# Down steps of a Strassen-Winograd pair: two PSUM banks in a fixed order, or five banks in a rotated order

## The reference

```
def swiglu(x, w_gate, w_up, w_down):
    return (jax.nn.silu(x @ w_gate) * (x @ w_up)) @ w_down
...
    h = x + 0.5 * swiglu(rmsnorm(x, ffn1_norm), ffn1_w_gate, ffn1_w_up, ffn1_w_down)
    p = rmsnorm(h, mix_norm) @ w_in
...
    h = h + jnp.concatenate([s_out, c_out.astype(s_out.dtype)], axis=-1) @ w_out
    h = h + 0.5 * swiglu(rmsnorm(h, ffn2_norm), ffn2_w_gate, ffn2_w_up, ffn2_w_down)
```

## Time and profile before

| | us |
|---|---|
| median of 3 runs | 1847.4 (1846.5 to 1847.51) |
| the profiled execution, whole | 1847.25 |
| its span, first to last instruction | 1845.4 |
| PE busy in it | 1792.8 (97%) |
| DVE busy | 1274.1 (69%) |
| ACT, POOL busy | 655.0, 624.0 |
| mean granted PE clock | 0.994 of full |

### The profile page before, as it was taken

One profiled execution on the slowest core, in us unless ns is written; L12 is line 12 of the kernel. 1 busy time (PEld: TensorE's weight loads), 2 busy tenths in 40 slices (PEclk: granted clock), 3 DMA queues, 4 the chain that ended last, 5 costly groups with the idle time before them and its releaser, 6 DMA issues.

```text
span 1845.4 us, 31589 instructions
## 1 busy us (share of the span) xinstructions
PE 1792.8 (97%) x11953; PEld 1751.7 (95%) x11953; DVE 1274.1 (69%) x2428; ACT 655.0 (35%) x1281; POOL 624.0 (34%) x669
## 2 busy tenths in 40 slices
PE   8999999999999999999999999899999999999998
PEld 7999999999999999999999999899999999999998
DVE  6658868677766865823774869767776686777766
ACT  7411333333333332533112455233233333333324
POOL 2787222322232222203994221233223223222321
PEclk9999999999999999999999999999999999999999
DMA  6133111111111110455114401111211111111112
GB/s 168 44 117 109 29 46 46 53 46 52 47 52 52 41 58 25 154 125 121 46 41 132 141 25 40 48 56 41 58 41 52 52 46 52 47 52 46 52 47 93
DMA packets 162502, 119.75 MB, mean 65 GB/s; under 512 B 10242, under 2 KB 156226, under 8 KB 161844
## 3 DMA queue, kind: packets, MB, share of 16 engines
q1 hardware_dynamic: 157012, 110.36, 20.3%
q0 software_dynamic: 864, 5.28, 0.9%
q10 hardware_dynamic: 4480, 2.10, 0.5%
HBM read 102.01 MB, written 15.72 MB: 64 GB/s over the span
## 4 chain that ended last, share of the span: by engine, by line
PE 92%; DVE 5%; issue 2%; ACT 1%; DMA 0%; DVEq 0%
PE bank_pair L1110 20%; PE bank_pair L1111 19%; PE bank_pair L1112 19%; PE bank_down L1110 11%; PE bank_down L1112 9%; PE bank_down L1111 9%; DVE HT L2262 1%; DVE XL L2285 1%; DVE XLX L2586 0%; PE bank_pair L1513 0%; PE bank_pair L1486 0%; PE bank_pair L1606 0%; PE bank_pair L1505 0%; DVE XTL L2574 0%; PE bank_pair L1218 0%
## 5 line engine op out<-in xcount | busy, mean ns | idle before, releaser
L2512 DVE SCALAR_TENSOR_TENSOR HT<-bank_down,HT 128x344 f32<-128x344 f32 x648 | 325.1, 513 | 166.1 <-PE bank_down L1112 163.1
L1110 PE MATMUL bank_pair<-XHM,U_hi 128*128 128x344 f32 x720 | 231.9, 322 | 1.9 <-issue 1.7
L1112 PE MATMUL bank_pair<-XHM,U_lo 128*128 128x344 f32 x720 | 230.0, 319 | 0.0
L1111 PE MATMUL bank_pair<-XLM,U_hi 128*128 128x344 f32 x720 | 229.9, 319 | 0.0
L3163 POOL TENSOR_TENSOR U_lo<-AST,U_hi 128x512 fp32r<-128x512 f32 x74 | 110.1, 1490 | 280.7 <-ACT U_hi L1670 280.7
L1110 PE MATMUL bank_pair<-XH,U_hi 128*128 128x344 f32 x608 | 195.4, 321 | 0.0
L1111 PE MATMUL bank_pair<-XL,U_hi 128*128 128x344 f32 x608 | 194.7, 320 | 0.0
L1112 PE MATMUL bank_pair<-XH,U_lo 128*128 128x344 f32 x608 | 194.5, 320 | 0.0
L1110 PE MATMUL bank_pair<-XH,WH 128*128 128x344 f32 x576 | 186.9, 325 | 4.4 <-DVE XL L2285 4.3
L1111 PE MATMUL bank_pair<-XL,WH 128*128 128x344 f32 x576 | 184.4, 320 | 0.0
L1112 PE MATMUL bank_pair<-XH,WL 128*128 128x344 f32 x576 | 184.3, 320 | 0.0
(11 more groups left out here) (375 smaller groups left out, 4583.2 us busy)
## 6 DMA issues: line engine op xcount, KB each, us to landing
DQ_raw<-in_ffn_w_down SPq DMA_DIRECT2D x52, 256.0 KB, 2.9
U_raw<-in_ffn_w_gate SPq DMA_DIRECT2D x40, 256.0 KB, 2.9
AST<-in_ffn_w_gate SPq DMA_DIRECT2D x40, 256.0 KB, 2.9
U_raw<-in_ffn_w_up SPq DMA_DIRECT2D x40, 256.0 KB, 3.3
AST<-in_ffn_w_up SPq DMA_DIRECT2D x40, 256.0 KB, 2.9
RAW<-in_w_in SPq DMA_DIRECT2D x16, 512.0 KB, 3.9
DQR<-in_ffn_w_down SPq DMA_DIRECT2D x25, 256.0 KB, 2.9
X<-in_x_prompt SPq DMA_DIRECT2D x8, 512.0 KB, 8.4
```

Source lines behind the costliest of these rows:

```text
L1110: pe.matmul(out, wh, xh, start=first, stop=False, skip_group_check=onto)
L1111: pe.matmul(out, wh, xl, start=False, stop=False, skip_group_check=onto)
L1112: return pe.matmul(out, wl, xh, start=False, stop=last, skip_group_check=onto)
L2512: dve.scalar_tensor_tensor(ht, DB[at % 2][:, 0:TW], 0.5, ht, ALU.mult, ALU.add).then_inc(pair_free, 1)
```

## The change

The steps of a quarter get a new order, M1, M5, M2, M6, M3, P1, M7, P2, and M4 goes behind M5 of the next quarter (the last M4 stands alone at the end, two steps behind the last M7). The steps use five banks in roles that change with the quarter: bank_down0 and 1, and the three banks of the up pass (bank_pair2's second half, bank_pair1's two halves), which no product uses in a gate pass. Each step waits for the add of the last step in its own bank. The up products V1a, M1 and M2 wait for the last adds on their banks. The first step goes behind product 7, and every product from there to 42 has exactly one. On DVE, an add stands two products later than its step (`ADD_LAG`); the last one falls into the up pass. The order of the hidden forms changes (`FORMS`, and `PLAIN_FORMS` for the first pair of an FFN), and on ACT three `sums_hi` move some places later.

```
-DOWN_STEPS = [((("W", A11, B11),), False, (0, 1)), ((("S", S1, T1),), False, (1, 2)),
...
-STEP_AFTER = [9 + 34 * n // STEPS for n in range(STEPS)]
-MIX_BEHIND = [len(DOWN_STEPS) * (q + 1) - 1 for q in range(3)]
+DOWN_STEPS = {"M1": ((("W", A11, B11),), False, (0, 1), 0), "M5": ((("S", S1, T1),), False, (1, 2), 1),
...
+DOWN_ORDER = []
+for _q in range(5):
+    for _name in ("M1", "M5", "M4", "M2", "M6", "M3", "P1", "M7", "P2"):
+        _at = _q - (_name == "M4")
+        if 0 <= _at < 4:
+            DOWN_ORDER.append((_at, _name))
+STEPS = len(DOWN_ORDER)
+BANK_ROLES = [(0, 1, 2, 3, 4), (2, 1, 3, 4, 0), (3, 1, 4, 0, 2), (4, 1, 0, 2, 3)]
+STEP_BANK = [BANK_ROLES[q][DOWN_STEPS[name][3]] for q, name in DOWN_ORDER]
+STEP_AFTER = [7 + n for n in range(STEPS)]
+ADD_LAG = 2
+QUARTER_LAST = [DOWN_ORDER.index((q, "M4")) for q in range(4)]
+MIX_BEHIND = QUARTER_LAST[:3]
 LOWS_BEHIND = [n + 4 for n in MIX_BEHIND]
-FORMS = [B13, B11, T1, T3, B22, B21, T4, T2, B23]
-PLAIN_FORMS = [B13, B11, T1, T3, B22, B23, B21, T4, T2]
+FORMS = [B13, B11, T1, B22, T2, B21, B23, T3, T4]
+PLAIN_FORMS = [B13, B11, T1, B22, B23, T3, B21, T2, T4]
...
+        STEP_BANKS = DB + [BANK[1][x] for x in ("v", "x", "y")]
...
-                out = bank_of(at)[:, 0:TW]
+                before = [i for i in range(n) if STEP_BANK[i] == STEP_BANK[n]]
+                if before:
+                    pe.wait_ge(pair_free, step_base(p) + before[-1] + 1)
+                elif STEP_BANK[n] >= 2:
+                    pe.wait_ge(h_raw, 6 * (p + 1))
+                elif p > 0:
+                    pe.wait_ge(pair_free, step_base(p))
+                else:
+                    pe.wait_ge(down_free, TILES * (DOWN1 + FO))
+                out = STEP_BANKS[STEP_BANK[n]][:, 0:TW]
...
+                if g == 1 and name in ("V1a", "M1", "M2"):
+                    bank = 2 + ("V1a", "M1", "M2").index(name)
+                    pe.wait_ge(pair_free, step_base(p - 1) + max(n for n in range(STEPS) if STEP_BANK[n] == bank) + 1)
...
                         unit_hi(t + 1, A11)
-                        sums_hi(4 * p - 2)
                         unit_hi(t + 1, A12)
                         copy_sum(t, "M6", (0, 2))
+                        sums_hi(4 * p - 2)
...
                     if g == 1:
+                        for n in range(STEPS):
+                            if STEP_AFTER[n] + ADD_LAG >= 4 * len(ORDER):
+                                step_add(p - 1, n)
                         dve.wait_ge(pair_full, step_base(p))
                     for i, name in enumerate(ORDER):
                         if g == 0:
                             for n in range(STEPS):
-                                if 4 * i <= STEP_AFTER[n] < 4 * i + 4:
+                                if 4 * i <= STEP_AFTER[n] + ADD_LAG < 4 * i + 4:
                                     step_add(p - 1, n)
```

More of the change, by code:

```diff
@@ L230, in copy_count @@
     return earlier(e, 0, len(COPIES)) + len(COPIES) * (n - 2) + COPIES.index(name) + 1
-DOWN_STEPS = [((("W", A11, B11),), False, (0, 1)), ((("S", S1, T1),), False, (1, 2)),
[L234 to L238, removed]
-STEP_AFTER = [9 + 34 * n // STEPS for n in range(STEPS)]
-MIX_BEHIND = [len(DOWN_STEPS) * (q + 1) - 1 for q in range(3)]
+DOWN_STEPS = {"M1": ((("W", A11, B11),), False, (0, 1), 0), "M5": ((("S", S1, T1),), False, (1, 2), 1),
+              "M2": ((("W", A12, B21),), False, (0, 1), 2), "M6": ((("S", S2, T2),), True, (0, 2), 0),
+              "M3": ((("S", S4, B22),), True, (0, 2), 1),
+              "P1": ((("W", A11, B13), ("W", A12, B23)), False, (0, 0), 3), "M7": ((("S", S3, T3),), True, (1, 2), 0),
+              "P2": ((("W", A21, B13), ("W", A22, B23)), False, (1, 0), 4), "M4": ((("W", A22, T4),), True, (1, 1), 0)}
+DOWN_ORDER = []
[11 more added lines that the diff above has]
+MIX_BEHIND = QUARTER_LAST[:3]
 LOWS_BEHIND = [n + 4 for n in MIX_BEHIND]
 BLOCK_OF = {B13: (0, 0), B11: (0, 1), B21: (1, 1), B22: (1, 2), B23: (1, 0)}
-FORMS = [B13, B11, T1, T3, B22, B21, T4, T2, B23]
-PLAIN_FORMS = [B13, B11, T1, T3, B22, B23, B21, T4, T2]
+FORMS = [B13, B11, T1, B22, T2, B21, B23, T3, T4]
+PLAIN_FORMS = [B13, B11, T1, B22, B23, T3, B21, T2, T4]
 MIXED = [T3, T1, T2, T4]
@@ L261, in quarter_end @@
     p, q = divmod(n, 4)
-    return step_base(p + 1) if p in LAST_PAIR else step_base(p) + len(DOWN_STEPS) * (q + 1)
+    return step_base(p + 1) if p in LAST_PAIR else step_base(p) + QUARTER_LAST[q] + 1
 def mixed_quarters(n):
@@ L1315, in pair_step @@
             def pair_step(p, n):
-                q, s = divmod(n, len(DOWN_STEPS))
-                parts, onto, _ = DOWN_STEPS[s]
+                q, name = DOWN_ORDER[n]
+                parts, onto, _, _ = DOWN_STEPS[name]
                 k = 4 * p + q
                 pe.wait_ge(dq_ready, k + 1)
-                at = step_base(p) + n
-                out = bank_of(at)[:, 0:TW]
+                before = [i for i in range(n) if STEP_BANK[i] == STEP_BANK[n]]
[8 more added lines that the diff above has]
+                out = STEP_BANKS[STEP_BANK[n]][:, 0:TW]
                 for x, (where, unit, form) in enumerate(parts):
@@ L1924, in ffn_passes @@
                         unit_hi(t + 1, A11)
-                        sums_hi(4 * p - 2)
                         unit_hi(t + 1, A12)
                         copy_sum(t, "M6", (0, 2))
+                        sums_hi(4 * p - 2)
                         quarter_hi(4 * p - 1)
                         unit_hi(t + 1, S1)
-                        sums_hi(4 * p - 1)
                         copy_sum(t, "M7", (1, 2))
@@ L1933, in ffn_passes @@
                         silu_sum(t, "C22", (1, 2))
+                        sums_hi(4 * p - 1)
                         unit_hi(t + 1, S3)
@@ L1936, in ffn_passes @@
                         quarter_hi(4 * p)
+                        silu_sum(t, "C12", (0, 2))
+                        silu(t, "M4", "x", (1, 1))
                         if p not in LAST_PAIR:
                             sums_hi(4 * p)
-                        silu_sum(t, "C12", (0, 2))
-                        silu(t, "M4", "x", (1, 1))
                         unit_hi(t + 1, S4)
@@ L2504, in step_add @@
             def step_add(p, n):
-                q, s = divmod(n, len(DOWN_STEPS))
-                _, onto, (m, tb) = DOWN_STEPS[s]
+                q, name = DOWN_ORDER[n]
+                m, tb = DOWN_STEPS[name][2]
                 at = step_base(p) + n
                 dve.wait_ge(pair_full, at + 1)
-                if DOWN_STEPS[s - 1][2] == (m, tb):
-                    dve.wait_ge(pair_free, at)
+                same = [i for i in range(n) if DOWN_ORDER[i][0] == q and DOWN_STEPS[DOWN_ORDER[i][1]][2] == (m, tb)]
+                if same:
+                    dve.wait_ge(pair_free, step_base(p) + same[-1] + 1)
                 ht = HT[:, 2 * q + m, block_cols(ffn_of(p), tb)]
-                dve.scalar_tensor_tensor(ht, DB[at % 2][:, 0:TW], 0.5, ht, ALU.mult, ALU.add).then_inc(pair_free, 1)
+                dve.scalar_tensor_tensor(ht, STEP_BANKS[STEP_BANK[n]][:, 0:TW], 0.5, ht, ALU.mult, ALU.add).then_inc(pair_free, 1)
             def mix_h(p, form):
```

## The result

The changed kernel takes 1871.6 us (median of 4 runs, 1870.15 to 1878.1), the kernel before beside it 1846.95 (4 runs, 1845.62 to 1847.51). The ratio is 1.0141, with a 95% interval of 1.0117 to 1.0166: slower by 24.6 us. The direction is the forecast one and the time lies inside the forecast range, but the move is more than twice the forecast 9.1 us. Nearly all of the difference comes from one term, quarter 2's entry.

What follows compares the result with a forecast made beforehand. PE was taken as the bound, leaving only gaps between its starts to win. Terms 9.8 - 4.8 + 4.7 - 1.8 + 1.2 = +9.1 us gave 1856.5 us, slower by 0.5%; 8-in-10 range 1838 to 1876.

Steps and rivals of the forecast that it cites:

- quarter 2's entry: Wait at quarter 2's M1, low parts against its deadline, late in five of 16 passes: +4.7 us.
- Start: M6 of quarter 0: first add 1.08 us later behind B23's low part, gap 1.25 for 0.64, +9.8 us.
- Middle: Mid-pass chained steps: three gaps (0.69 us) go, 0.39 appears at M1 of quarter 3, -4.8 us over 16 passes.
- the five late passes: Passes where A12 comes late at quarter 2: wait 0.2 to 0.7 us, or 1.4 each if POOL's S1 goes first.
- the row of 546.53: DVE row before the change, read as a rule: DVE's next low part, 0.68 us, passes a waiting POOL.
- the rival: POOL's S1 goes between quarter 2's two low parts, 1.3 us more each pass, 1877 us; chance 0.13.
- End: Last M4 of quarter 3: add 33 at t + 8.0 after product M3, gap 1.35 for 1.46, -1.8 us.
- the same six gaps: Claim that all 16 ordinary gate passes before the change show six gaps at chained steps, 2.8 us a pass.
- First passes: First gate pass of each FFN: given the start term of ordinary passes, 2 x 0.6 = +1.2 us.
- The costless parts: Listed at no cost: V1a, M1, M2 bank waits, step 2's bank, up pass's last add, sums_hi behind silu, later loads.

Runs made afterwards that it cites:

- experiment 2: Changed kernel with hidden forms T3 and T4 ahead of B23 again, B23 last as before the change: 1857.7 us, ratio 1.0045 to the kernel before.
- 7: Changed kernel with unit S2's low part moved on DVE from ahead of a gate pass's first add to behind that window's adds: 1864.9 us, ratio 1.0096.
- Experiment 1: Changed kernel with DVE's two low parts of a quarter swapped, the quarter's own ahead of the sums': 1841.1 us, ratio 0.9964 to the kernel before.
- experiment 6: Changed kernel with the high part of quarter 2's weights made on ACT before unit A12's high part: 1874.6 us, ratio 1.0145 to the kernel before.
- experiment 8: Changed kernel with the quarter's low part ahead of the sums', T3 and T4 ahead of B23, a quarter's last low parts behind add 33: 1805.7 us, 0.9777.
- experiment 5: Changed kernel with the high part of quarter 2's sums put back ahead of unit A12's high part on ACT: 1848.6 us, ratio 1.0012.
- the best kernel: The kernel of experiment 8 with quarter 2's sums_hi ahead of A12 and unit S2's low part behind the first adds: 1797.4 us, ratio 0.9733.
- experiment 10: Kernel before, two banks and old step order kept, with the low parts of units S2 and S3 moved behind adds on DVE: 1816.2 us, ratio 0.9837.

## Why the prediction had the sign right and the order at the port wrong

**Start.** Right: M6 of quarter 0 at 1.24 us (1.25 forecast), and the first add at 486.41, behind the forms in the order that was worked out. Experiments 2 and 7 show that it is DVE's queue ahead of the first add and nothing else.

**Middle.** Right in kind: the chained waits are gone and M1 of quarter 3 is late instead, 0.48 for 0.39. Experiment 1 shows that the sums' low part ahead of the quarter's is all of it.

**Quarter 2's entry.** This term failed, 19.0 us for 4.7. The timetable up to it was good: I had put M1's deadline and the low parts' end within 0.1 us of each other. The step that failed is the one in which POOL's S1 "would be first there" only in the five late passes, and in the sum at half weight, since in the row of 546.53 a waiting POOL was passed by DVE's next. In that row POOL asks 0.07 us before DVE's next starts, and so it does, by 0.06 or 0.07 us, in all 16 ordinary passes of before: one near tie repeated 16 times, not 16 cases of a rule. In 14 passes of the changed kernel and the 13 of experiment 6, POOL asks 0.04 to 0.44 us before DVE's next, while the sums' low part runs, and in all of them it is served first. The pass of 1570.54, where DVE is 0.01 us ahead, goes the other way.

The trace of before had the counter-example too, in each of its 16 ordinary passes, and the prediction read half of it. At 538.60 POOL asks while DVE's instruction of 537.85 runs; POOL's grows to 1.57, which the forecast used, and DVE's next, 0.44 us behind the request, takes 1.49 where its like at 540.46 takes 0.51, which it left out:

```profile
537.85 1.16 DVE L2569 TENSOR_TENSOR HR<-HR,S 128x344 f32<-128x344 f32 x1
539.04 1.49 DVE L2533 TENSOR_TENSOR XTR<-HR 128x344 f32<-128x344 f32 x1
540.46 0.51 DVE L2533 TENSOR_TENSOR HR<-HR 128x344 f32<-128x344 f32 x1
```

By the Trainium skill, page "SBUF — State Buffer", section "🔬 SBUF: two separate sides", whichever of the two starts first keeps the shared pair for the whole instruction; the strict reading of it, which I had put down as the rival, agrees with these rows and not with the tie.

What decides a tie stays open. At the place of 546.53, behind a low part of 344 columns and 0.06 to 0.08 us ahead of DVE's next, POOL came second in all 16 ordinary passes of before, but first in one of 16 in experiment 2 and in one of 16 in experiment 8 (535.36 above). In the first pass of an FFN, also behind a low part of 344 columns, POOL asks 0.06 us ahead and comes first, in both such passes of before. POOL, then DVE:

```profile
213.40 2.79 POOL L3163 TENSOR_TENSOR U_lo<-AST,U_hi 128x512 fp32r<-128x512 f32 x2 [13.83 <-ACT U_hi L1670]
```

```profile
213.03 0.51 DVE L2574 TENSOR_TENSOR HL<-T,HH 128x344 fp32r<-128x344 f32 x1
213.46 3.11 DVE L2574 TENSOR_TENSOR XTL<-XTR,XTH 128x344 fp32r<-128x344 f32 x2
```

So the width of the instruction ahead is not what tells the cases apart, and the row of 546.53 was no rule.

The second half of the error: I took A12's landing as a matter of a few late passes, and the low parts as just in time. But POOL's request lies 18.0 us behind the first step in every pass, the first low part 17.4 to 17.8 in the 14 punctual passes and the second 18.0 to 18.4, so 13 of them were on the wrong side. A quantity that the forecast put at a tie should have had the price of its bad side in the sum, 16 x 1.1 us, or a chance near one half, not 0.13.

**End.** M4 of quarter 3 came to 1.26 (1.35 forecast). The two last passes of the FFNs have no sums to mix and no gap, which is most of the 3.4 us between forecast and measurement. Before, these two had no gap at M4 either, so "the same six gaps" holds for 14 passes.

**First passes.** The prediction put their waits before at 6.9 us above an ordinary pass; counted again in the same trace it is 6.0 and 5.5, which touches its bounds and not the sum. I gave them the start's term; they got the entry's too (1.06 and 2.51), and M2 of quarter 0 waits 0.9 and 1.1 us for B21's low part.

**The costless parts.** The waits of V1a, M1 and M2 on the step banks show no gap. The `sums_hi` behind the silu, listed there too, shows no gap of its own. The one of quarter 2 stood in the entry's chain instead, and its move behind A12 cost 23 us (experiment 5): the chain's end was held against M1's deadline and not against POOL's request.

## What to carry to other kernels

Where DVE and POOL share a port, list the requests of both in time, not only their loads: an instruction of POOL that falls into the first of two two-input instructions of DVE adds about 1.1 us to the second. Put first the one that is needed first, and put something that reads PSUM behind it. Before more banks are given to a chain, look at what stands ahead of the add that frees the bank: two moved lines were worth 30 us here, the five banks with their order and the other edits 19. And where a trace shows a race won 16 times by the same 0.07 us, it is one observation.

## What the runs showed of the hardware that was not expected

The clock after an idle stretch was not a matter of its length alone. In the best kernel both first passes idle ahead of M6 of quarter 0, PE:

```profile
218.38 0.63 PE L1121 MATMUL bank_down<-XTH,SH 128*128 128x344 f32 x1 [2.22 <-DVE HT L2535]
...
1137.56 0.40 PE L1121 MATMUL bank_down<-XTH,SH 128*128 128x344 f32 x1 [2.21 <-DVE HT L2535]
```

and the windows behind them:

```profile
218.20:223.00 4.80, 4.62 (x16) 4.65 (x17) 3.07 (x7) 0.65 (x2) 0.79 (x1) 0.50 0.40 114
1137.30:1141.50 4.20, 3.94 (x25) 3.98 (x26) 3.66 (x8) 0.73 (x2) 0.86 (x1) 1.00 0.48 137
```

After 2.22 us the granted clock is 0.50, the 1.2 GHz level, and after 2.21 us it stays at 1.00, 2.4 GHz. What PE did ahead of them differs (M2 of quarter 0 had waited 0.87 and 1.10 us). In the kernel of experiment 10, at the same place of the first FFN, PE idles longer, 2.39 us ahead of 217.17, and the window 217:222 has 1.00. And two ordinary passes of the changed kernel, whose last 6 us look alike (PE busy 3.92 and 3.81 us at a clock of 1.00), part in the same way:

```profile
571.16 0.66 PE L1121 MATMUL bank_pair<-HH,DQH 128*128 128x344 f32 x1 [2.25 <-DVE DQL L2501]
...
1391.44 0.42 PE L1121 MATMUL bank_pair<-HH,DQH 128*128 128x344 f32 x1 [2.22 <-DVE DQ_lo L2501]
```

```profile
571.20:574.50 3.30, 3.30 (x12) 3.30 (x13) 1.63 (x4) 0.00 (x0) 0.00 (x0) 0.50 0.00 0
1391.50:1394.80 3.30, 3.30 (x21) 3.30 (x22) 1.75 (x4) 0.22 (x1) 0.17 (x1) 1.00 0.00 0
```

What makes the difference stays open; no run here separates it.
